# Head norms summed by rounds of three tiles, a stacked decay sum, and a memory attention by pairs of heads

## The chip, the cores and the metric

One core of a Trainium2 chip runs the kernel. The metric is the device time of one execution in microseconds (us); smaller is better. TensorE multiplies, VectorE, ScalarE and GpSimd work on tiles in SBUF and PSUM, and SyncE (SP) issues the loads of the weights.

## The reference, cut to what matters

Two blocks of a model over 512 tokens of width 1024, in f32. The first has three mixers (a state-space scan with decays per head, a gated recurrence, retention) and a feed-forward; the second has two layers with memory attention in both and multi-head latent attention in the second.

```python
def rms_norm(x, g):
    y = xf * lax.rsqrt(jnp.mean(xf * xf, axis=-1, keepdims=True) + EPS)
    return y * g
def memory_attention(q_mem, mem, mem_norm_g, w_mem_kv, g_q, g_k):
    q = rms_norm(q_mem.reshape(b, s, 4, 64), g_q)
    k, v = jnp.split(rms_norm(mem, mem_norm_g) @ w_mem_kv, 2, axis=-1)
    k = rms_norm(k.reshape(b, m, 4, 64), g_k)
    p = jax.nn.softmax(jnp.einsum('bqhd,bmhd->bhqm', q, k) * 64 ** -0.5, axis=-1)
    o = jnp.einsum('bhqm,bmhd->bqhd', p, v)
```

There are 256 memory tokens (m). The latent attention has 6 heads; for each, rms_norm is applied to the 128 plain features of keys and queries and to their 64 rotary ones, before rotation; the attention is causal over both parts.

The decay sums are the running sums of log decays of each of 16 heads along the tokens; the first block needs exp of their differences within a chunk of 128 tokens.

## The kernel before, in words

Activations lie as tiles of 128 features by 512 tokens. Every weight is f32 and is split in two f32r halves: ScalarE copies the raw panel to w_hi (L1366), VectorE (L1871) or GpSimd (L649) subtracts to get w_lo, and TensorE does three matmuls per block (L689 to L691). A panel is 128 by 1024, eight blocks; 525 panels are streamed by SP into four raw buffers, each load waiting for the low of the panel four before it; w_hi and w_lo have two buffers each, so ScalarE starts panel n when TensorE is done with panel n - 2. STAGES (L64 on) lists the stages with their panels, tiles and posting units. POOL_RUNS (L96) names the runs of panels whose lows GpSimd makes; VectorE makes the others. The order of all work on each engine is written out by hand in the four engine programs, and semaphores with counts join them. There is no planner.

PSUM has eight banks: 0 to 3 take the GEMM tiles in turn (bank_free waits until tile t - 4 was drained), 4 to 7 are the AUX banks, taken in turn by aux_tile (L768 on); aux_done, aux_used count their filling and use.

**Decay sums.** In stage ssd_y the sums of 16 heads stand in rows (acs, 16 by 512). They are split into acs_hi and acs_lo (VectorE, L2252), and spread(hd) (L949) broadcasts the row of one head over 128 partitions by two matmuls, one of each half, with a column of the identity (L954, L955). Two heads are spread between two gate panels; ScalarE and VectorE make the decay matrices from them.

**Small norms.** A head norm needs the mean of squares over the 128 or 64 features of a head, for each token. sums (L779) multiplies the squares of a tile, 128 tokens at a time as the stationary operand, by one column of ones (L788, two columns for 64-wide heads), so that the sums stand by token in a few columns. ScalarE takes the root of these columns (L1421), VectorE the reciprocal (L2007, 0.2 us), and spread_norms (L794) turns them back with the identity over the features (L804). VectorE multiplies the tile by gain and norm (L2013). ROUNDS (L140) lists ten rounds of two tiles in the second layer: keys, memory queries, queries, rotary parts, memory keys. Squares are ScalarE's there (L1414).

**First layer.** After conv0 the memory queries (qm0) are projected, then the norm of the memory itself, the panels of mem0 (four of 256 columns, the memory's keys and values), then conv, nine panels whose tiles VectorE combines in conv_part (L2535) by threes. Between them TensorE does the sums and spreads of the memory keys and of the memory queries, turns the values (L1124), and runs Attention: eight units, each one head by 256 queries. A unit is scores (L1131), maximum on VectorE (L2022), exponential on ScalarE (L1444), division on VectorE (L2041), transposition (L854), copy on ScalarE, and the values of a head after its two units (L1137). Unit u is done after conv panel u + 2; the last ones follow the last conv panel and stand in wo0's first tile.

**Second layer.** mla_in gives cq (three tiles) and the memory queries qm. ukv (three panels) gives keys and values of the six heads; the values are turned (L1222) in six PSUM tiles of a stage of their own. uq (five panels) gives six q_nope and three q_rope tiles, mem1 (four panels) the memory's keys and values. The rounds of norms stand between the panels. VectorE normalises the memory again (L2518 on), from a second sum of squares (ScalarE's eight squares, L1762, and TensorE's memory_sum1, L821) and makes the rotary tables (L2675 to L2685); ScalarE takes their sine (L1822). turn (L1227) does the rotation of a tile. Then pairs of heads run in STEPS: memory pairs and latent pairs by PairedHeads (L240), whose two heads use the two halves of the array's rows or columns (L1259, L1306).

Of the kernel before, what the change touches and what calls it, by code (L numbers as in the profile page):

```python
# [26 lines left out]
F32 = mybir.dt.float32  # L27
F32R = mybir.dt.float32r
# [56 lines left out]
def schedule():  # L85
    out, n, t, s = {}, 0, 0, 0
    for name, panels, tiles, units in STAGES:
# [9 lines left out]
             "conv": (ST["conv0"].n + 2, ST["wo0"].n), "s1a": (ST["s1a_in0"].n + 2, ST["s1a_in"].n - 1),  # L97
# [34 lines left out]
def split_runs():  # L132
# [7 lines left out]
ROUNDS = [["k0", "k1"], ["k2", "k3"], ["k4", "k5"], ["mq0_1", "mq1_1"], ["q0", "q1"], ["q2", "q3"], ["q4", "q5"],  # L140
          ["qr0", "qr1"], ["mk0_1", "mk1_1"], ["qr2"]]
SMALL_NORMS = [(f"m{w}{j}_0", 1, MEM_D, c, False, (2, 3)) for w, c in (("k", MEM), ("q", S)) for j in range(2)]
SMALL_NORMS += [("ckv", 2, 2 * P, S, False, (0, 1, 2, 3)), ("krope", 1, 64, S, False, (0, 1, 2, 3)),
                ("cq", 3, 3 * P, S, False, (0, 1, 2, 3))]
SMALL_NORMS += [(name, 1, P if name[1].isdigit() else 64, MEM if name[:2] == "mk" else S, True, (0, 1, 2, 3))
                for names in ROUNDS for name in names]

# [10 lines left out]
def small_norms():  # L158
    out, squared, rotation = {}, {True: DT, False: 0}, 0
    for rooted, (name, tiles, dim, cols, by_scalar, slots) in enumerate(SMALL_NORMS):  # L160
        n = SmallNorm()
        n.tiles, n.dim, n.cols, n.by_scalar, n.heads = tiles, dim, cols, by_scalar, P // dim if dim < P else 1
        n.slots = [slots[(rotation + j) % len(slots)] for j in range(tiles)]
        n.squared = [squared[by_scalar] + j + 1 for j in range(tiles)]
        n.rooted = rooted + 1
        first = 8 * (rooted % 8)
        n.stats = slice(first, first + n.heads * cols // P)
        rotation, squared[by_scalar] = rotation + tiles, squared[by_scalar] + tiles
        out[name] = n
    return out  # L170
# [32 lines left out]


class Attention:

    def __init__(self, sems, heads, chunks, u0, t0, width, scale, pairs, probs, p_tok, scores, turned, outs, lag, stat,
                 cat):
        (self.scored, self.max_ready, self.exp_done, self.prob_ready, self.pt_done, self.pt_copied, self.pv_done,
         self.pv_taken) = sems
        self.heads, self.chunks, self.u0, self.t0, self.width, self.scale = heads, chunks, u0, t0, width, scale
        self.pairs, self.probs, self.p_tok, self.scores, self.turned = pairs, probs, p_tok, scores, turned
        self.outs, self.lag, self.stat, self.cat = outs, lag, stat, cat
        self.per_head = CH // chunks
        self.n, self.ahead = heads * self.per_head, len(scores)  # L220

    def tile(self, hd):

        return (hd // 2, hd % 2 == 0, hd % 2 == 1) if self.pairs else (hd, True, True)

    def due(self, u, more):

        at_unit = [self.per_head * (hd + 1) + self.lag + more for hd in range(self.heads)]
        return [hd for hd, x in enumerate(at_unit) if x == u or u == self.n - 1 < x]

    def columns(self, u, which, e=None):

        c = self.stat + 4 * which + u * self.chunks % 4
        return slice(c, c + self.chunks) if e is None else slice(c + e, c + e + 1)

    def prob(self, u):
# [2636 lines left out]
```

## Time and profile before

| | |
|---|---|
| median of three runs | 3074.87 us (3074.26 to 3077.01) |
| the profiled execution | 3075.68 us |
| its span, first to last instruction | 3073.9 us |
| TensorE busy | 3027.8 us, 99% |
| VectorE, ScalarE, GpSimd busy | 59%, 31%, 8% |
| mean granted TensorE clock | 0.994 |
| HBM read | 283.96 MB, 93 GB/s |

The table is of the whole span. TensorE's time is that of its matmuls with their ends modelled, so that neighbours overlap; the spacing of their starts is what an edit changes.

### The profile page before, as it was taken

The numbers are of one execution on the slowest core, as the hardware profiler recorded it, in microseconds if no ns is written. First come the engines' busy times: TensorE is split into PE (matmuls) and PEld (weight loads), VectorE is DVE, ScalarE is ACT, GpSimd is POOL, SyncE is SP. The second block draws the span as 40 slices with busy tenths as digits, with TensorE's granted clock in tenths as the row PEclk, the third lists the DMA queues.
The fourth block names the chain that finished last, engine by engine and source line by source line (L and its number), as shares of the span: only waits on it lengthen the run. The fifth ranks groups of instructions, "written<-read, shape, count | busy, mean of one in ns | idle before, by whom it ended". The sixth has DMA issues, their size and how long they took to land.

```text
span 3073.9 us, 36959 instructions
## 1 busy us (share of the span) xinstructions
PE 3027.8 (99%) x13711; PEld 2467.5 (80%) x13711; DVE 1815.4 (59%) x2422; ACT 946.4 (31%) x1302; POOL 243.6 (8%) x111
## 2 busy tenths in 40 slices
PE   8999999999999999999999999999999999999999
PEld 7887788787888878888777888887888878688887
DVE  8896565667666555554666655445554447665532
ACT  4643632333222222222223222222222234422222
POOL 0043240000000000000142000002000022000000
PEclk9999999999999999999999999999999999999999
DMA  4222123233222222223321222332222321022222
GB/s 145 96 96 83 62 96 117 69 104 102 96 96 98 100 96 82 96 99 106 110 96 62 91 100 96 103 103 89 97 99 98 108 81 56 28 96 96 96 102 97
DMA packets 79309, 287.61 MB, mean 94 GB/s; under 512 B 8992, under 2 KB 9248, under 8 KB 78816
## 3 DMA queue, kind: packets, MB, share of 16 engines
q1 hardware_dynamic: 77904, 280.06, 27.1%
q0 software_dynamic: 1296, 6.03, 0.6%
q8 instruction: 76, 1.25, 0.2%
q14 instruction: 33, 0.27, 0.0%
HBM read 283.96 MB, written 2.10 MB: 93 GB/s over the span
## 4 chain that ended last, share of the span: by engine, by line
PE 85%; issue 9%; DVE 3%; POOL 2%; ACT 1%; DMA 0%; POOLq 0%; DVEq 0%; ACTq 0%
PE ps L689 26%; PE ps L690 26%; PE ps L691 26%; POOL w_lo L649 2%; PE ps L788 1%; PE ps L804 1%; PE ps L1071 1%; PE ps L1268 0%; PE ps L1319 0%; DVE w_lo L1871 0%; PE ps L1296 0%; ACT w_hi L1366 0%; PE ps L753 0%; PE ps L1271 0%; PE ps L1060 0%
## 5 line engine op out<-in xcount | busy, mean ns | idle before, releaser
L1366 ACT ACTIVATE w_hi<-raw 128x1024 fp32r<-128x1024 f32 x524 | 554.4, 1058 | 1366.5 <-PE ps L691 1366.2
L689 PE MATMUL ps<-h_hi,w_hi 128*128 128x512 f32 (+1 forms) x2379 | 934.3, 393 | 7.0 <-DVE w_lo L1871 3.3
L690 PE MATMUL ps<-h_lo,w_hi 128*128 128x512 f32 (+1 forms) x2379 | 924.3, 389 | 0.0
L691 PE MATMUL ps<-h_hi,w_lo 128*128 128x512 f32 (+1 forms) x2379 | 924.2, 389 | 0.0
L1871 DVE TENSOR_TENSOR w_lo<-raw,w_hi 128x1024 fp32r<-128x1024 f32 x430 | 525.8, 1223 | 470.6 <-ACT w_hi L1366 465.4
L689 PEld LDWEIGHTS ps<-h_hi,w_hi 128*128 128x128 f32 x2379 | 448.1, 188 | 111.9 <-issue 10.9
L691 PEld LDWEIGHTS ps<-h_hi,w_lo 128*128 128x128 f32 x2379 | 447.8, 188 | 92.6
L690 PEld LDWEIGHTS ps<-h_lo,w_hi 128*128 128x128 f32 x2379 | 448.1, 188 | 91.9 <-issue 2.2
L689 PE MATMUL ps<-mid_hi,w_hi 128*128 128x512 f32 x1208 | 471.6, 390 | 2.2 <-DVE mid_lo L1949 2.1
L690 PE MATMUL ps<-mid_lo,w_hi 128*128 128x512 f32 x1208 | 470.5, 389 | 0.0
L691 PE MATMUL ps<-mid_hi,w_lo 128*128 128x512 f32 x1208 | 470.4, 389 | 0.0
L649 POOL TENSOR_TENSOR w_lo<-raw,w_hi 128x1024 fp32r<-128x1024 f32 x94 | 236.2, 2513 | 953.4 <-ACT w_hi L1366 945.7
L689 PEld LDWEIGHTS ps<-mid_hi,w_hi 128*128 128x128 f32 x1208 | 227.2, 188 | 51.3 <-DVE mid_lo L1949 3.5
L691 PEld LDWEIGHTS ps<-mid_hi,w_lo 128*128 128x128 f32 x1208 | 227.1, 188 | 47.3
L690 PEld LDWEIGHTS ps<-mid_lo,w_hi 128*128 128x128 f32 x1208 | 227.2, 188 | 47.1 <-issue 0.2
L1944 DVE TENSOR_TENSOR stage<-ps,rstd 128x512 f32<-128x512 f32 x104 | 71.8, 691 | 233.7 <-PE ps L691 233.7
L1371 ACT ACTIVATE stage<-ps 128x512 f32<-128x512 f32 x107 | 63.6, 599 | 365.2 <-PE ps L691 352.1
L689 PE MATMUL ps<-br_hi,w_hi 128*128 128x512 f32 x256 | 101.5, 397 | 10.0 <-DVE br_lo L2083 7.9
L1944 DVE TENSOR_TENSOR tmp<-ps,rstd 128x512 f32<-128x512 f32 x73 | 50.4, 691 | 99.5 <-PE ps L691 99.3
L690 PE MATMUL ps<-br_lo,w_hi 128*128 128x512 f32 x256 | 100.6, 393 | 0.0
L691 PE MATMUL ps<-br_hi,w_lo 128*128 128x512 f32 x256 | 100.6, 393 | 0.0
L1692 ACT ACTIVATE tmp<-tmp 128x512 f32<-128x512 f32 x112 | 69.3, 619 | 72.0 <-DVE tmp L1967 58.2
(416 smaller groups left out, 2556.6 us busy)
## 6 DMA issues: line engine op xcount, KB each, us to landing
raw<-in_wstream SPq DMA_DIRECT2D x525, 512.0 KB, 3.3
x<-in_x SPq DMA_DIRECT2D x4, 512.0 KB, 6.4
x_in<-in_x POOLq DMA_DIRECT2D x8, 256.0 KB, 3.0
mem_x<-in_mem POOLq DMA_DIRECT2D x2, 1024.0 KB, 5.0
out<-x SPq DMA_DIRECT2D x8, 256.0 KB, 4.4
tmp<-in_ret_decay POOLq DMA_DIRECT2D x1, 1024.0 KB, 5.9
rope_r<-in_rope_r POOLq DMA_DIRECT2D x1, 512.0 KB, 4.0
mats<-in_mats SPq DMA_DIRECT2D x1, 256.0 KB, 8.3
```

The costliest lines, as they stand in the source:

```text
L649: nc.gpsimd.tensor_tensor(w_lo[:, n % HL], raw[:, n % RAW], w_hi[:, n % HL].bitcast(F32), ALU.subtract)\
L689: nc.tensor.matmul(dst, hi_w, hi_x, start=first, stop=False)
L690: nc.tensor.matmul(dst, hi_w, lo_x, start=False, stop=False)
L691: return nc.tensor.matmul(dst, lo_w, hi_x, start=False, stop=last)
L788: mm = nc.tensor.matmul(dst[:, n.heads * c:n.heads * c + n.heads], tmp[:, n.slots[j], P * c:P * c + P], ones, start=j == 0, stop=j == n.ti ...
L804: mm = nc.tensor.matmul(dst[rows, P * c:P * c + P], small[:, k:k + 1].to_broadcast([P, P // n.heads]), IDENT, start=True, stop=True)
L1071: mm = nc.tensor.matmul(bank(t)[:, P * c:S], v_tok[:, c, f:f + P], scores[:, hd % 2, OFF[c]:OFF[c] + WIDTH[c]], start=c == 0, stop=True, s ...
L1366: nc.scalar.activation(w_hi[:, n % HL], raw[:, r], ACT.Copy).then_inc(hi_ready, 1)
L1371: nc.scalar.activation(dst, src[rows, 0:cols], func, bias=bias, scale=scale).then_inc(drained, 1)
L1692: nc.scalar.activation(tmp[:, s % 2], tmp[:, s % 2], func).then_inc(act_done, 1)
L1871: v.tensor_tensor(w_lo[:, n % HL], raw[:, n % RAW], w_hi[:, n % HL].bitcast(F32), ALU.subtract)\
L1944: v.tensor_tensor(dst, bank(t), scale, ALU.mult).then_inc(drained, 1)
```

## The change

1. Decay sums: acs_hi and acs_lo become rows 0 to 15 and 32 to 47 of one tile of 64 rows, zero elsewhere, and a table pick2 of two stacked identities selects both at once: one matmul for a head.
2. Rounds: a round is three tiles. round_sums sums the squares over the partitions, with 32 columns of ones, into three groups of 32 partitions of one bank; ScalarE takes one root of 96 by 512, VectorE one reciprocal, and round_spread broadcasts them over the features in three banks, from three groups of 32 rows, six matmuls for 64-wide heads. Seven rounds: one in the first layer, six in the second. Memory keys (two tiles of 256) count as one tile.
3. First memory attention: PairedHeads in four steps, scores and first transposition in the middle of a conv panel.
4. Lows of memory panels 1 to 3 and of conv panel 0 go from GpSimd to VectorE; mem0's first low stays.
5. Second layer: the panels of uq and mem1 and the turned values are interleaved in one stage with the rotary query tiles earlier; the reciprocal root of the memory is kept from the first layer (L1762 and L821 go); rotary tables and sine come earlier; the AUX banks of the pairs are renamed.

Removed with them are the class Attention, sums of these tiles and spread_norms of them. The core of the diff, in the order of the file: tables, TensorE (helpers, first layer, second layer), ScalarE's root, VectorE (reciprocal, first layer, second layer):

```diff
-    ("mla_in", 5, 5, 0), ("ukv", 3, 12, 0), ("v_turned", 0, 6, 0), ("uq", 5, 9, 0), ("mem1", 4, 4, 0), ("wo1", 8, 8, 8),
+    ("mla_in", 5, 5, 0), ("ukv", 3, 12, 0), ("uq", 9, 19, 0), ("wo1", 8, 8, 8),
-             "conv": (ST["conv0"].n + 2, ST["wo0"].n), "s1a": (ST["s1a_in0"].n + 2, ST["s1a_in"].n - 1),
+             "conv0": (ST["conv0"].n + 2, ST["mem0"].n), "conv": (ST["conv"].n + 1, ST["wo0"].n), "s1a": (ST["s1a_in0"].n + 2, ST["s1a_in"].n - 1),
+MEM1_PANEL, MEM1_TILE = (2, 3, 7, 8), (10, 11, 17, 18)
+UQ_PANEL, UQ_TILE = (0, 1, 4, 5, 6), (2, 3, 6, 7, 12, 13, 14, 15, 16)
+V_TILE = (0, 1, 4, 5, 8, 9)
+ROUNDS = [["mq0", "mq1", "mk"], ["k0", "k1", "k2"], ["k3", "k4", "k5"], ["mq0", "mq1", "mk"], ["qr0", "qr1", "qr2"], ["q0", "q1", "q2"],
+          ["q3", "q4", "q5"]]
...
+            def round_sums(r):
+                dst, heads = aux_tile(), len(ROUNDS[r])
+                ones = ONES[:, 0:32] if by_head(r) else mat["ones64"][:, 48:80]
+                pe.wait_ge(act_squared, DT + heads * r + heads)
+                for j in range(heads):
+                    mm = nc.tensor.matmul(dst[32 * j:32 * j + 32, :], ones, square_slot[square_of(r, j)], start=True, stop=True)
                 mm.then_inc(aux_done, 1)
+            def round_spread(r):
+                pe.wait_ge(aux_used, sum_at[r])
+                dst = [aux_tile() for _ in ROUNDS[r]]
+                wide = P if by_head(r) else 64
+                for first in range(0, P, wide):
+                    for j in range(len(ROUNDS[r])):
+                        rows, one = slice(32 * j, 32 * j + 32), 32 * j + first // 4
+                        mm = nc.tensor.matmul(dst[j][first:first + wide, :], IDENT[rows, one:one + 1].to_broadcast([32, wide]),
+                                              rows_rstd[r % 2][rows], start=True, stop=True)
...
-                nc.tensor.matmul(dst, sel, acs_hi[:], start=True, stop=False)
-                nc.tensor.matmul(dst, sel, acs_lo[:], start=False, stop=True).then_inc(bcast_done, 1)
+                nc.tensor.matmul(spread_bank(hd), pick2[:, hd:hd + 1].to_broadcast([64, P]), acs2[:], start=True, stop=True)\
+                    .then_inc(bcast_done, 1)
...
+            round_sums(0)
+            for j in range(2):
+                memory_turned(ST["mem0"].t + 3 + j, mem_vt, j)
             conv_part(ST["conv"], 1)
+            round_spread(0)
+            def middle(j):
+                if j == 5:
+                    first_values(1)
+                if j < 6:
+                    first_scores(j - 2)
+                if 3 <= j < 7:
+                    first_turned(j - 3, 0)
+                if j == 7:
+                    first_values(3)
+            for j in range(2, 9):
+                conv_part(ST["conv"], j, middle=(lambda: middle(j)) if j < 8 else None)
+                if 3 <= j < 7:
+                    first_turned(j - 3, 1)
...
+            round_sums(1)
+            v_turned_tiles(0)
+            uq_gemm(0)
+            round_spread(1)
+            round_sums(2)
+            v_turned_tiles(2)
+            uq_gemm(1)
+            round_spread(2)
+            v_turned_tiles(4)
+            mem1_gemm(0)
+            mem1_gemm(1)
+            uq_gemm(2)
+            round_sums(3)
+            uq_gemm(3)
+            round_spread(3)
+            round_sums(4)
+            uq_gemm(4)
+            round_spread(4)
+            round_sums(5)
             turn(krope[:, 0])
+            mem1_gemm(2)
+            round_spread(5)
+            round_sums(6)
+            normalised(4)
+            turn(q_rope[:, 0])
+            mem1_gemm(3)
+            round_spread(6)
...
+                nc.scalar.activation(rows_rstd[r % 2], ps[0:96, AUX + (aux[0] - 1) % 4], ACT.Sqrt, bias=eps_col[0:96],
+                                     scale=1.0 / (P if by_head(r) else 64)).then_inc(rows_rooted, 1)
...
+                v.reciprocal(rows_rstd[r % 2], rows_rstd[r % 2]).then_inc(aux_used, 1)
...
+            split(ST["mem0"].n + 1)
             conv_part(ST["conv1"], 2, 2, 2)
-            for j in range(4):
+            for j in range(1, 4):
                 split(ST["mem0"].n + j + 1)
+            conv_part(st, 3, 0, 3)
+            round_reciprocal(0)
+            for j in range(2):
+                memory_values(mem_v, j)
             conv_part(st, 3, 1, 3)
+            round_norms(*memory_gain("q", 0), qm[:, 0], qm[:, 1])
+            round_norms(*memory_gain("k", 0), mem_k_whole)
...
+            rotary_table(0, 0.25)
+            rotary_table(1, 0.0)
+            reciprocals("cq")
+            memory_input(1, mem_x1, spare[:, 0], mem1_hi, mem1_lo, range(0, 4))
+            small_norm("cq", [cq[:, k] for k in range(3)], [vcol("g_q_lora_2", k) for k in range(3)])
+            for k in range(3):
+                halves(cq_hi[:, k], cq_lo[:, k], cq[:, k], lat_ready if k == 2 else None)
+            round_reciprocal(1)
+            memory_input(1, mem_x1, spare[:, 0], mem1_hi, mem1_lo, range(4, 8))
+            round_norms(gk, *(k_nope[:, hd] for hd in range(3)))
+            round_reciprocal(2)
+            round_norms(gk, *(k_nope[:, hd] for hd in range(3, 6)))
+            round_reciprocal(3)
+            round_norms(*memory_gain("q", 1), qm[:, 0], qm[:, 1])
+            round_norms(*memory_gain("k", 1), mem_k1_whole)
+            round_reciprocal(4)
+            round_norms(gr, *(q_rope[:, j] for j in range(3)))
+            round_reciprocal(5)
+            turn(krope[:, 0])
+            round_norms(gq, *(q_nope[:, hd] for hd in range(3)))
+            round_reciprocal(6)
+            turn(q_rope[:, 0])
+            round_norms(gq, *(q_nope[:, hd] for hd in range(3, 6)))
```

## Rows read from the trace of the kernel before

**Rows 1.** The page: busy time, two groups of part 5, an issue of part 6
```profile
PE 3027.8 (99%) x13711; PEld 2467.5 (80%) x13711; DVE 1815.4 (59%) x2422; ACT 946.4 (31%) x1302; POOL 243.6 (8%) x111
...
L1871 DVE TENSOR_TENSOR w_lo<-raw,w_hi 128x1024 fp32r<-128x1024 f32 x430 | 525.8, 1223 | 470.6 <-ACT w_hi L1366 465.4
...
L649 POOL TENSOR_TENSOR w_lo<-raw,w_hi 128x1024 fp32r<-128x1024 f32 x94 | 236.2, 2513 | 953.4 <-ACT w_hi L1366 945.7
...
raw<-in_wstream SPq DMA_DIRECT2D x525, 512.0 KB, 3.3
```

**Rows 2.** Windows: start:end, length, busy us of PE, PEld, DVE, ACT, POOL, clock, DMA
```profile
294.88:364.80 69.92, 69.92 (x398) 52.01 (x398) 38.56 (x68) 50.08 (x118) 17.17 (x7) 1.00 0.17 54
...
1570.64:1677.65 107.01, 97.15 (x494) 75.84 (x492) 64.58 (x102) 30.34 (x65) 32.71 (x13) 0.95 0.20 68
...
2495.83:2597.42 101.59, 98.04 (x686) 85.52 (x684) 57.17 (x98) 47.00 (x87) 29.53 (x12) 0.98 0.20 67
```

**Rows 3.** Windows of two stretches at the lower clock, same columns
```profile
1579.90:1586.70 6.80, 4.74 (x22) 4.74 (x23) 4.80 (x2) 0.47 (x1) 4.52 (x2) 0.50 0.37 122
1607.20:1610.60 3.40, 3.26 (x10) 2.71 (x11) 1.46 (x6) 1.41 (x2) 2.37 (x1) 0.50 0.01 2
```

**Rows 4.** TensorE's waits, 1570 to 1678: us in total, times, longest
```profile
PE ps L689 <- POOL w_lo L649: 6.2, 3, 4.3
```

**Rows 5.** Timeline, TensorE: start, us, engine, line; 256 and 512 columns
```profile
1587.00 0.28 PE L689 MATMUL ps<-mem_hi,w_hi 128*128 128x256 f32 x1
...
1587.36 0.28 PE L689 MATMUL ps<-mem_hi,w_hi 128*128 128x256 f32 x1
...
2488.35 0.39 PE L689 MATMUL ps<-h_hi,w_hi 128*128 128x512 f32 x1
...
2489.03 0.39 PE L689 MATMUL ps<-h_hi,w_hi 128*128 128x512 f32 x1
```

**Rows 6.** Timeline, TensorE: from one pair's first spread to the next work
```profile
308.50 0.49 PE L954 MATMUL ps<-acs_hi,ident_r 16*128 16x512 f32 x1
...
309.63 0.50 PE L689 MATMUL ps<-h_hi,w_hi 128*128 128x512 f32 x1
```

**Rows 7.** Chain that ended last, in order of time: start, us, what
```profile
420.22 0.86 PE ps L753 x2
...
1625.83 1.06 PE ps L1131 x4
...
1648.38 1.86 PE ps L1137 x4
...
2612.20 1.87 PE ps L1306 x8
...
2614.44 1.06 PE ps L1259 x8
```

**Rows 8.** Timeline of VectorE, GpSimd and ScalarE at six places
```profile
2466.53 3.35 DVE L1938 RECIPROCAL rstd<-rstd 128x512 f32<-128x512 f32 x1
...
1572.38 2.59 DVE L2546 TENSOR_TENSOR cpad<-tmp,stage 128x512 f32<-128x512 f32 x1
...
2517.68 1.75 DVE L2511 RECIPROCAL rstd<-rstd 128x256 f32<-128x256 f32 x1
...
2517.09 2.93 POOL L649 TENSOR_TENSOR w_lo<-raw,w_hi 128x1024 fp32r<-128x1024 f32 x1 [9.40 <-ACT w_hi L1366]
...
2588.09 1.28 ACT L1822 ACT_TABLE_LOAD   x1
2589.39 1.06 ACT L1822 ACTIVATE rope<-rope 128x1024 f32<-128x1024 f32 x1
```

**Rows 9.** Groups of TensorE from 2495.8 to 2597.4: busy us, mean ns
```profile
L788 PE MATMUL ps<-mats,tmp 128*128 128x1 f32 (+1 forms) x168 | 19.7, 247 | 0.0
...
L804 PE MATMUL ps<-mats,small 128*128 128x128 f32 (+1 forms) x200 | 19.0, 276 | 0.6 <-DVE small L2007 0.6
```

**Rows 10.** Timeline, VectorE: the first score maximum of the second layer
```profile
2597.42 0.68 DVE L2709 TENSOR_REDUCE small<-ps 128x2 f32<-128x512 f32 x1
```

More of the change, by code:

```diff
@@ L202, in col @@
     return vec[:, c:c + 1] if i is None else vec[:, bass.ds(i * step + c, 1)]
[L205 to L236, printed above, removed]
-        return self.probs[:, u % self.probs.shape[1]]
 class PairedHeads:
@@ L829, in att_start @@
-            def att_start(a, score, tiles):
-                pe.wait_ge(aux_used, aux[0])
-                pe.wait_ge(rms_done, norms[0])
-                pe.wait_ge(drained, tiles)
-                for u in range(a.ahead):
-                    att_scores(a, score, u)
-            def att_value(a, value, hd):
-                tile, first, last = a.tile(hd)
-                pe.wait_ge(a.pt_copied, a.u0 + a.per_head * (hd + 1))
-                if first and tile >= len(a.outs):
-                    pe.wait_ge(a.pv_taken, a.t0 + tile - len(a.outs) + 1)
-                mm = value(a.outs[tile % len(a.outs)], hd)
-                if last:
-                    mm.then_inc(a.pv_done, 1)
@@ new lines, in side_rows, with memory_scores @@
+            def side_rows(side):
+                return slice(64 * side, 64 * side + 64)
+            def memory_scores(a, keys, k, dst):
+                j = a.pair(k)
+                for e in range(2):
+                    for side in range(2):
+                        mm = nc.tensor.matmul(dst[side][:, MEM * e:MEM * e + MEM], qm[side_rows(side), j, a.queries(k, e, 1)],
+                                              keys[side_rows(side), j], start=True, stop=True)
+                        if e == 1:
+                            mm.then_inc(a.scored, 1)
@@ L1722, in _, with memory @@
                     memory_root(spare[:, 0])
-            def memory(l, k, v_in, behind=None):
+            def memory(l, k, v_in):
                 st = ST[f"mem{l}"]
@@ new lines, in uq_drain, with mem1_drain, drained_up_to @@
+            def uq_drain(g):
+                n = st.n + UQ_PANEL[g]
+                split(n + 1)
+                for k in range(2 * g, min(2 * g + 2, 9)):
+                    drain(n, st.t + UQ_TILE[k], q_rope[:, k - 2] if 2 <= k < 5 else q_nope[:, k if k < 2 else k - 3])
+            def mem1_drain(j):
+                n = st.n + MEM1_PANEL[j]
+                split(n + 1)
+                drain(n, st.t + MEM1_TILE[j], mem_k1[:, j] if j < 2 else mem_vt1[:, j - 2], cols=MEM)
+            def drained_up_to(tile):
+                act.wait_ge(drained, st.t + tile + 1)
```

599 lines of the change are left out of this document (241 added, 358 removed).

## The prediction

> **What bounds the kernel now.** I read the page's busy line first: TensorE is busy 99% of the span [rows 1], so a change is worth what it takes off TensorE's own queue, plus or minus TensorE's waits. Then the windows of the three stretches that are edited [rows 2]: the spread of the decay sums, from 294.88; the memory GEMMs and the first attention, from 1570.64 to the second output tile of wo0 at 1677.65; and the second layer's norms, from ukv at 2495.83 to the first score maximum at 2597.42 [rows 10]. TensorE is busy all of the first, 97.15 of 107.01 us of the second and 98.04 of 101.59 us of the third. The granted clock falls in the second: 6.8 us from 1579.9 and 3.4 us from 1607.2 stand at half speed [rows 3], which costs (6.8+3.4)/2 = 5.1 us. TensorE is idle for 107.01 - 97.15 = 9.9 us there, 6.2 of them waiting for weight lows made by GpSimd [rows 4].
>
> A spacing is what TensorE pays: for a weight block of 512 columns 0.68 us by its three matmuls, so 5.46 us a panel of eight; with 256 columns 0.36 us, so 2.9 us a panel [rows 5]. An f32 matmul of the code stands as two records.
>
> **Decay sums.** Each pair of heads issues four matmuls in 1.13 us, from 308.50 to 309.63 [rows 6]. Each streams 0.23 us; the remaining 0.2 us lies at the ends, where the array's row grouping changes. Two matmuls leave 1.13 - 0.46 = 0.67 us. Eight pairs give **-3.7 us**. The fill and the pick table (VectorE, some 0.5 us) come before spread(0), which is due only about 1 us after the lows are ready: hidden; at worst +0.5. ScalarE is busy 50.08 of 69.92 us [rows 2], so it need not become the bound.
>
> **Overlap of narrow matmuls.** Nothing in the trace runs three at once; it shows two. Scores of one head take 1.06 us for four records, of two heads on alternate row halves 1.06 us for eight; values of one head take 1.86 us for four records, of two heads on alternate column halves 1.87 us for eight [rows 7]. A plain f32 matmul of 512 columns takes 0.86 us [rows 7]. So a round's sum (three matmuls on three column groups) costs between 1.0 us (all at once, with 0.1 for the change of grouping) and 3 x 0.86 = 2.6 us (one by one); its spread the same, for 64-wide heads (six matmuls) 1.5 to 5.2 us. I take 1.0, 1.0 and 1.5, as the rows with two are twice as fast to within 0.01 us.
> The Trainium skill, "TensorEngine Tiling (Array Packing)", Key Properties, says that different tiles can execute in parallel, and its table of speedups goes to four for a dimension of 32 or less. By it the low ends hold; by the pair rows alone, read as a limit of two, a round's sum would be 1.7 to 1.9 us. No row here shows three.
>
> **First attention.** TensorE's new content from 1570.64: four memory panels 11.9, nine conv panels and one tile of wo0 54.6, round sum 1.0, two turned values 0.6, round spread 1.5, four paired scores 4 x 1.06 = 4.2, eight transpositions as before 4.2, two paired values 3.7: together 81.7 us. Old content: the same GEMMs 66.5, scores 8 x 1.06, values 4 x 1.86, transpositions 4.2, and sums, spreads and turned values of some 6.2, so 92.8 us; with 9.9 idle and 5.1 of slow clock that is 107.8, against 107.0 measured.
> The waits, laid out in queue order. Lows of memory panels 1 to 3 and of conv panel 0 leave GpSimd (2.51 us [rows 1], and it blocks VectorE's SBUF work: a product took 2.59 us beside it where others take 0.7 [rows 8]) for VectorE (1.23 us [rows 1]). But the first is queued behind a conv part: VectorE's product, scale and two taps end at 1575.0, the low at 1576.3, so memory panel 1, with panel 0 done at 1573.6, waits 2.8 us. The low of panel 2 is ready at 1579.9: 0.7 us. Conv panel 0 starts at 1586.0 instead of 1591.04. Round 0: sum at 1591.4, root, and then a reciprocal of 512 columns, 3.35 us [rows 8], in place of 0.18 us ones: done at 1596.8, the spread at 1598.5 doesn't wait. VectorE then does conv part (3,1), one of its operations held 2.3 us by GpSimd, and three norms: ready at 1606.6, while the first scores stand ready at 1602.7: **a new wait of 4.0 us**. Behind the waiting scores stand the rest of conv panel 2 and all later panels. Later steps have 7 us a panel for a chain of 4 us; wo0 waits some 0.4. Waits total 7.9, against 9.9. So 81.7 + 7.9 = 89.6, tile 1 of wo0 at 1660.2: -17.4 us. I add one half-clock stretch of 3.4 us, 1.7 us, where the old had three: **-15.7**.
>
> **Second layer.** The old stretch holds 168 records of column sums and 200 of spreads [rows 9]; 19.7 + 19.0 = 39 us with the parts for cq; the memory's square sum is some 3 more. New content: ukv 18.1 with its half-clock stretch as before, cq's sum and spread 3.5, six round sums 6.0, four spreads of 1.0 and two of 1.5, six turned v tiles 3.2, nine uq tiles 18.4, four memory panels 11.9, two rotary turns 1.9, one turned value 0.3: 70.3 us. ScalarE's eight squares and the sum for the memory go (the reciprocal root of the first layer is reused), off the path but for 3.3 us of TensorE.
> VectorE's queue decides the waits. The rotary tables (16 operations, 10 to 12 us with one or two GpSimd holds) now stand ahead of cq, as do four memory tiles (4.7 us), so cq's lows end at 2522.6. ScalarE's sine moves before uq's first split: table 1.28 and sine 1.06 us [rows 8]; it delays that panel's hi, which is ready anyway, and the table returns before root 1. The six reciprocals add 6 x 3.35 = 20 us. In order, TensorE waits: round sum 1 for squares 0.9; uq panel 0 for cq 2.3; spread 2 for its reciprocal, behind memory tiles and three norms, 4.4; memory panel 1 for its low 1.3; uq panel 3 for a drain 0.9; spread 4 2.6, spread 5 0.7, spread 6 2.2 for their reciprocals. That is 15.3 us. Scores 0 start at 2495.8 + 70.3 + 15.3 = 2581.4. VectorE then still turns one rotary tile, norms three and copies one (after the reciprocal ended at 2580.0): first maximum at 2584.4, with old 2597.42: -13.0; the loose ends of the queues take 0.7, so -12.3. One more half-clock stretch, 1.7: **-10.6**. What follows (pairs) has the same steps and is moved whole; a value copy between two maxima costs 0.4 at most.
> SP's loads wait for lows as before; four loads ahead at 3.3 us each [rows 1] cover panels of 3 to 5.5 us. Unrolled loops of SP and GpSimd: nothing.
>
> **Sum.** 3.7 + 15.7 + 10.6 = 30.0. The profiled execution took 3075.68 us; the median of the three runs is 0.8 below it. 3075.68 - 30.0 = 3045.7, median-like **3045**.
>
> **Rivals.**
> A. *Three narrow matmuls don't overlap.* With 0.86 each the second layer is 2.8 us slower than now, the first attention gains 15.9, decay 3.7; with 3.4 for the clock -13.4: 3062. Against: the pair rows. Chance 0.10.
> B. *Slower: each narrow f32 matmul also empties the array before the next group's.* Place: the 51 matmuls of the seven rounds. At 1.2 us each the gain is 1.7 less 3.4 for the clock, about nothing; each 0.1 us more costs 5.1. At 1.4 us each: +8 to +10, 3084. It decides from 1.3 us. Against: alternate halves show no such price [rows 7]. Chance 0.03, and 0.03 for a price near 1.2, no change.
> The Tiling page of the Trainium skill, Key Properties, says that changing the tiling mode, not just the tile, drains the engine; by that B would not occur, only one entry and exit a round. The 0.2 us of rows 6 fit that.
> C. *VectorE is later still.* If reciprocals were held by GpSimd too, 1.2 us each, the second layer's waits grow by 5: 3050 to 3052. Against: a reciprocal of 256 columns at 2517.68 took its 1.75 us while GpSimd was on [rows 8]. Chance 0.16.
> D. *Fewer waits than laid out and no half-clock stretches.* 3.4 back and half of the 15.3 covered: 3034 to 3037. Chance 0.12.
> E. *The change of lows does nothing*, as VectorE only swaps the wait: panel 0 of conv at 1590 instead of 1586: 3049, inside the range.
>
> **How the numbers follow.** Forecast with E 0.56. The range 3033 to 3063 leaves out B and the tails. A measurement tells 0.2%, 6 us, from no change. Faster by more: all but B and a little, 0.94; within 0.03; slower 0.03.
>
> **What would show it.** In the profile after: decay pairs of 0.67 us; round sums and spreads near 1.0 us (2.6 shows A); conv panel 0 near 1586; waits before the first scores of about 4 us and before spread 2 of about 4, both ended by VectorE; records on TensorE fewer by some 450; first maximum of the second layer 13 us earlier relative to ukv. Wrong if a wait over 5 us stands in either stretch, or if half clock covers over 20 us more.

## The result, and the profile after

The changed kernel takes **3041.84 us** (median of four runs, 3039.88 to 3043.62), the kernel before, run between them on the same chip, 3075.57. The ratio is 0.989, its 95% interval 0.9873 to 0.9907: 34 us less. Timed again beside three of the experiments, the changed kernel took 3042.61 against 3074.76, ratio 0.9894 (0.9877 to 0.991). The forecast was 3045, the range 3033 to 3063. The profiled execution took 3040.44 us with a span of 3038.2; the span of before was 3073.9.

The page of the changed kernel: busy time of each engine, and the two groups of lows [rows 1].

```profile
PE 2986.5 (98%) x13373; PEld 2418.5 (80%) x13373; DVE 1828.8 (60%) x2405; ACT 943.8 (31%) x1279; POOL 231.7 (8%) x107
...
L1846 DVE TENSOR_TENSOR w_lo<-raw,w_hi 128x1024 fp32r<-128x1024 f32 x434 | 530.7, 1223 | 473.9 <-ACT w_hi L1344 473.1
```

TensorE has 338 records fewer and 41.3 us less busy time, but the span fell by 35.7: the rest became waiting. The windows of the same three stretches [rows 2] (start:end, length, busy us of PE, PEld, DVE, ACT, POOL, granted clock, DMA share, GB/s) are these.

```profile
294.74:367.72 72.98, 72.62 (x414) 54.41 (x413) 41.20 (x73) 51.69 (x121) 19.87 (x8) 1.00 0.16 53
1565.92:1658.16 92.24, 85.17 (x440) 66.00 (x438) 64.06 (x98) 31.59 (x64) 21.95 (x9) 0.96 0.24 79
2474.88:2562.61 87.73, 76.04 (x412) 54.18 (x410) 68.24 (x82) 45.83 (x72) 28.99 (x12) 0.94 0.23 77
```

The second line was 107.01 us long and is 92.24; the third was 101.59 and is 87.73. In the third TensorE was idle 3.6 us and is idle 11.7 now, although the stretch is 13.9 shorter: the part took off more than 20 us of work and gave 8 back in waits. The first window is cut later than the one of before, by which the stage with the decay sums ended at 370.96; now it ends at 367.72.

The table places the whole difference by where stretches begin and end in the two traces.

| where | before | after | difference |
|---|---|---|---|
| end of the stage with the decay sums | 370.96 | 367.72 | -3.24 |
| up to memory panel 0 (a half-clock stretch at 1173.7 is absent) | 1570.64 | 1565.92 | -4.72, so -1.5 more |
| memory GEMMs and first attention | 107.01 | 92.24 | -14.77 |
| between (a half-clock stretch at 2129.4 is absent) | 818.18 | 816.72 | -1.46 |
| second layer up to the first maximum | 101.59 | 87.73 | -13.86 |
| pairs of heads up to wo1 | 69.28 | 68.66 | -0.62 |

They sum to 35.4 of 35.7 us. Half clock means a granted clock of 0.50 in the rows, 1.2 GHz, the lower of TensorE's two levels. The two absent stretches, 3.0 us, stand where the programs agree, each behind a wait that both kernels have (2.06 us, ended at 1173.8 in the kernel before and at 1170.5 in the changed one, and 1.88 us, ended at 2128.4 and at 2108.9). They are no part of the change and come and go from run to run: in the second profile of the changed kernel half clock stands at 1144.0 and 1171.3, and the memory panels start at 1568.10 instead of 1565.92.

The new waits of TensorE in the second stretch, and then in the third (engine, tile, line, what it waited for: us in total, times, longest), are:

```profile
PE ps L822 <- DVE mem_k L2024: 3.7, 1, 3.7
PE ps L663 <- DVE w_lo L1846: 3.3, 2, 2.8
```

```profile
PE ps L809 <- DVE ckv L2019: 6.5, 3, 3.6
PE ps L663 <- issue: 2.0, 1, 2.0
PE ps L797 <- DVE krope L2649: 1.2, 1, 1.2
PE ps L663 <- POOL w_lo L622: 0.7, 2, 0.4
PE ps L1101 <- issue: 0.7, 1, 0.7
PE ps L797 <- ACT stage L1392: 0.6, 1, 0.6
```

L822 are the scores, L809 the spreads of a round, L797 its sums, L663 the GEMMs, L1101 a turned tile. Where GpSimd's lows ended 6.2 us of waiting before [rows 4], VectorE's norms and lows end 7.0 now.

TensorE's timeline shows what the narrow matmuls cost (start, us, engine, line, tiles, count): a decay pair, then round 0's sum, then its spread of six matmuls.

```profile
302.77 0.73 PE L935 MATMUL ps<-acs,pick 64*128 64x512 f32 x2
303.43 1.13 PE L957 MATMUL ps<-xw_tok,b_tok 128*128 128x512 f32 x2
...
1587.63 0.62 PE L797 MATMUL ps<-tmp,mats 128*32 128x512 f32 x2
1587.64 0.62 PE L797 MATMUL ps<-acc,mats 128*32 128x512 f32 x1
1588.08 0.60 PE L797 MATMUL ps<-tmp,mats 128*32 128x512 f32 x2
1588.09 0.59 PE L797 MATMUL ps<-acc,mats 128*32 128x512 f32 x1
1588.62 0.33 PE L1101 MATMUL ps<-mats,mem_vt 128*128 128x128 f32 x1
...
1594.69 1.10 PE L809 MATMUL ps<-ckv,mats 32*64 32x512 f32 x12
1595.72 0.50 PE L663 MATMUL ps<-h_hi,w_hi 128*128 128x512 f32 x1
```

A pair takes 303.43 - 302.77 = 0.66 us instead of 1.13 [rows 6]. In the sum, the first records of all three matmuls start within 0.01 us at 1587.63, the second records at 1588.08, and the next work at 1588.62: 0.99 us for three matmuls of 0.86 each. The six of the spread take 1.03 us.

### The profile page after: what moved, and what is told of

The parts are those of the page before. It is cut to its first block, busy times and chain, and to the rows that moved or that the text cites. A ratio compares the mean times of both kernels' runs of the same rounds, so it can differ in the third digit from the quotient of the medians.

```text
span 3038.2 us, 36195 instructions
## 1 busy us (share of the span) xinstructions
PE 2986.5 (98%) x13373; PEld 2418.5 (80%) x13373; DVE 1828.8 (60%) x2405; ACT 943.8 (31%) x1279; POOL 231.7 (8%) x107
## 4 chain that ended last, share of the span: by engine, by line
PE 83%; issue 10%; DVE 5%; POOL 2%; ACT 1%; DMA 0%; POOLq 0%; ACTq 0%; DVEq 0%
PE ps L663 26%; PE ps L665 26%; PE ps L664 26%; POOL w_lo L622 2%; PE ps L1052 1%; PE ps L1297 0%; DVE w_lo L1846 0%; PE ps L1260 0%; DMA mem_x<-in_mem 0%; ACT w_hi L1344 0%; PE ps L833 0%; PE ps L727 0%; PE ps L1041 0%; DVE small L1997 0%; PE ps L947 0%
## 5 line engine op out<-in xcount | busy, mean ns | idle before, releaser
L663 PE MATMUL ps<-h_hi,w_hi 128*128 128x512 f32 (+1 forms) x2379 | 935.1, 393 | 8.7 <-DVE w_lo L1846 3.3
L663 PEld LDWEIGHTS ps<-h_hi,w_hi 128*128 128x128 f32 x2379 | 448.4, 188 | 115.7 <-issue 13.5
L663 PE MATMUL ps<-mid_hi,w_hi 128*128 128x512 f32 x1208 | 470.8, 390 | 2.2 <-DVE mid_lo L1924 2.1
L622 POOL TENSOR_TENSOR w_lo<-raw,w_hi 128x1024 fp32r<-128x1024 f32 x90 | 224.3, 2493 | 939.8 <-ACT w_hi L1344 931.8
L663 PEld LDWEIGHTS ps<-mid_hi,w_hi 128*128 128x128 f32 x1208 | 226.8, 188 | 50.8 <-DVE mid_lo L1924 3.5
L663 PE MATMUL ps<-br_hi,w_hi 128*128 128x512 f32 x256 | 101.8, 398 | 9.7 <-DVE br_lo L2060 7.7
```

The lines of the kernel that those rows point to most:

```text
L622: nc.gpsimd.tensor_tensor(w_lo[:, n % HL], raw[:, n % RAW], w_hi[:, n % HL].bitcast(F32), ALU.subtract)\
L663: nc.tensor.matmul(dst, hi_w, hi_x, start=first, stop=False)
```

## The experiments

All were made from the changed kernel; the diffs are cut to their core. Two measures are used beside the medians: the memory stretch, from memory panel 0 to the second output tile of wo0 (92.24 us, in its second profile 92.26), and the norm stretch, from the first column sum of cq (2480.34) to the first maximum (82.27, in its second profile 83.33). A median of the changed kernel is 3041.84 or 3042.61, and its single runs lie between 3039.88 and 3043.62, so that a part worth 1 us shows in its place and not in a median. The second profile of the changed kernel has the waits of the first at the same places, but half clock at other ones.

### The decay sum in two matmuls again

```diff
-nc.tensor.matmul(spread_bank(hd), pick2[:, hd:hd + 1].to_broadcast([64, P]), acs2[:], start=True, stop=True)
+nc.tensor.matmul(dst, sel, acs_hi[:], start=True, stop=False)
+nc.tensor.matmul(dst, sel, acs_lo[:], start=False, stop=True)
```

> The change without its decay part: each decay spread is again two matmuls, of the high half and of the low half. My theory (the seven later pairs of spreads stand in TensorE's line with nothing beside them): a pair of spreads goes from 0.66 back to 1.13 us, the stage with the heads ends 3.2 to 3.7 us later, and the kernel takes 3.2 to 3.7 us more than the changed one, with everything behind it only moved. Rival (the vector work of the stage sets its end, and TensorE would wait there for as long as it saved): the pair is 1.13 us again but the stage ends less than 1 us later.

Measured: a pair takes 1.13 us (294.38 to 295.51), the stage runs from 294.38 to 370.46, 3.1 us longer than the 294.74 to 367.72 of the changed kernel, and memory panel 0 starts 2.66 us later. The median is 3043.23. The stage comes within 0.1 us of the theory's 3.2 to 3.7 and the rival falls. The medians differ by 0.6 to 1.4 us only, where the expectation had 3.2 to 3.7: in the total this part is not shown, as half-clock stretches at other places move the medians by as much.

### Round sums one by one

```diff
-for j in range(heads):
+for j in range(heads if by_head(r) else 0):
+    mm = nc.tensor.matmul(dst[0:96, :], shifted[:, 64 - 32 * j:160 - 32 * j], square_slot[square_of(r, j)],
+                          start=j == 0, stop=j == heads - 1)
+for j in range(0 if by_head(r) else heads):
     mm = nc.tensor.matmul(dst[32 * j:32 * j + 32, :], ones, ..., start=True, stop=True)
```

> The sums of the four rounds whose heads are 128 wide (rounds 1, 2, 5, 6) are made by three full-height matmuls that add up in one bank, each with its ones shifted to its 32 columns, so that no two can run beside each other; the values are the same. My theory (three matmuls in three column groups of 32 run beside each other, which is why a sum took 0.99 us): a sum takes 2.5 to 2.7 us, 1.6 more each, 6.4 in all, of which 4 to 6.4 us show in the total, since a longer sum also starts the root and the reciprocal behind it later, while the waits in front of uq0 and of round sum 6 take in some. Rival (a sum is short because its matmuls write only 32 rows, and not because they overlap): a full-height one differs from it too, so that the length alone would not tell; what tells is the spacing of the starts, 0.02 to 0.1 us inside a sum now and 0.86 us in this kernel.

Here shifted is a tile of zeros with 32 columns of ones, so that each matmul writes all 96 rows and the three add up in one bank.

Measured: 3046.19 us, 3.6 to 4.4 more than the changed kernel, and a norm stretch of 87.30 (2479.46 to 2566.76), 4.0 to 5.0 longer. TensorE's timeline of round sum 1 here:

```profile
2496.50 1.07 PE L797 MATMUL ps<-tmp,fill 128*96 128x512 f32 x2 [0.63 <-ACT stage L1395]
2497.41 1.88 PE L797 MATMUL ps<-stage,fill 128*96 128x512 f32 x4
2499.13 1.04 PE L1213 MATMUL ps<-mats,q_nope 128*128 128x128 f32 x8
2500.74 0.47 PE L663 MATMUL ps<-h_hi,w_hi 128*128 128x512 f32 x1 [0.57 <-issue]
```

The sum now takes 2499.13 - 2496.50 = 2.63 us for the same three inputs, with starts 0.9 us apart, where those of the changed kernel are 0.01 us apart. Running beside each other is thus what makes a sum 0.99 us. Four sums are 6.6 us longer and not all of it shows: the wait at uq0, behind the sum, fell from 1.97 to 0.57, that at spread 2 from 3.58 to 1.99. Rival A of the prediction had this for every round.

### The two heads in turn

```diff
-for e in range(2):
-    for side in range(2):
+for side in range(2):
+    for e in range(2):
```

and the same exchange in the values.

> The memory attentions with the same matmuls in another order: both halves of the scores of one head and then both of the other, and likewise the four value matmuls of one head and then those of the other (before and after the change the heads alternate matmul by matmul). My theory (the two heads' matmuls lie in different halves of the array, and run beside each other only when they stand next to each other in the queue): scores go from 1.06 to about 1.7 to 2.1 us a step and values from 1.87 to about 3.0 to 3.7, with 8 steps of each in the two layers together 10 to 22 us, of which the last value step of one head may still overlap the next thing. Rival (the queue looks past its head, so order does not matter): scores and values as before, and the total within 1 us.

Measured: 3040.49 us, memory stretch 92.30. Scores 1.08 us, values 1.87: nothing changed. **The theory was wrong in its condition.** That the two heads overlap isn't touched, since one head's two value matmuls alone took 1.86 us in the kernel before [rows 7] and four take 1.87 here; but they need not alternate.

### In turn, with a wait between

```diff
 for side in range(2):
+    pe.wait_ge(a.pt_copied, a.count(k, 1))
     for c in range(MEM // P):
```

> As the kernel with the heads in turn, with one more wait on a semaphore long reached, between the value matmuls of the first head and those of the second, so that the order in which they are handed to TensorE is certain. Theory (TensorE starts a record that waits for nothing in its own half of the array while earlier ones still run in the other half, up to some records ahead): a value step again takes 1.87 us. Rival (in the earlier experiment the matmuls had been brought back into alternating order before they reached TensorE): 2.6 to 3.5 us a value step, as the wait holds the order.

Measured: 3041.67 us, and this value step in TensorE's timeline:

```profile
1628.14 1.94 PE L842 MATMUL ps<-p_tok,mem_v 128*64 128x512 f32 x8
1630.02 1.14 PE L822 MATMUL ps<-mem_k,qm 64*128 64x256 f32 x8
```

1630.02 - 1628.14 = 1.88 us. Eight records (four of one head, then four of the other) still take the time of four. The trace bears out that the program kept its edit: two of the step's weight loads carry the wait, and in both kernels with the heads in turn the first records of the two heads start 13 to 14 ns apart, where they start 6 ns apart when the heads alternate. The rival, alternating order brought back ahead of TensorE, is thus very unlikely, though no row shows the queue itself. It is then TensorE that starts the second head's records beside the first's. How far ahead it does so was not tried beyond these four records.

### The four lows on GpSimd again

```diff
-"conv0": (ST["conv0"].n + 2, ST["mem0"].n), "conv": (ST["conv"].n + 1, ST["wo0"].n)
+"conv": (ST["conv0"].n + 2, ST["wo0"].n)
```

> The change without the move of the four lows: those of memory panels 1 to 3 and of convolution panel 0 of the last channel tile are made by GpSimd again, at 2.9 us each, instead of VectorE. My theory (GpSimd's chain of lows, 2.9 us each, stands ahead of these panels, and with TensorE's work in between made shorter it would be late): memory panels 1, 2 and 3 wait for it, convolution panel 0 starts 3 to 5 us later than in the changed kernel, and since VectorE is relieved of 4 x 0.6 us and of the waits for the highs, the first scores wait less than 3.75 us; net 1 to 4 us slower. Rival (the lows are no bound once the round is short): memory panel 1 waits as now, convolution panel 0 starts within 0.5 us of now, and the total is within 1 us or even lower, since VectorE's norms for the first scores come sooner.

The list of runs that GpSimd makes is back to one run from conv0 on.

Measured: 3045.93 us, 3.3 to 4.1 more. The waits of its memory stretch (96.91 us, from 1566.33):

```profile
PE ps L662 <- POOL w_lo L622: 5.8, 3, 4.3
PE ps L821 <- DVE mem_k L2023: 3.7, 1, 3.7
PE ps L662 <- DVE w_lo L1845: 0.5, 1, 0.5
```

Convolution panel 0 starts 20.68 us after memory panel 0 instead of 16.13. The 5.8 us are nearly the 6.2 of before [rows 4]. Rival E (moving the lows does nothing) falls. The wait of the scores did not shrink, against what I had expected: it is counted from the round sum, which came as much later as the panels did.

### Three orders of VectorE's queue

Norms of round 0 ahead of a convolution part:

```diff
-conv_part(st, 3, 1, 3)
 round_norms(*memory_gain("q", 0), qm[:, 0], qm[:, 1])
 round_norms(*memory_gain("k", 0), mem_k_whole)
...
         maxima(mem_first, j - 2, side, FIRST_SCORES[side])
+    if j == 2:
+        conv_part(st, 3, 1, 3)
```

> In VectorE's queue the norms of round 0 (memory queries and keys) stand before the second part of convolution tile 3, which goes behind the first pair's maxima. My theory (the 3.75 us at the first scores are VectorE's: the reciprocal of 3.35 us, a conv part, one operation of it held by GpSimd, and three norms): the wait at the first scores falls to 0.5 to 1.5 us, the part is still in time for its panel, and the kernel takes 2 to 3.5 us less. Rival (the reciprocal alone makes the lateness): the wait stays above 2.5 us and the total falls by less than 1.2 us.

The lows of memory panels 1 and 2 ahead of the taps:

```diff
-conv_part(ST["conv1"], 2, 1, 2)
-split(ST["mem0"].n + 1)
-conv_part(ST["conv1"], 2, 2, 2)
-for j in range(1, 4):
+for part in (1, 2):
+    scaled(ST["conv1"].n + part, ST["conv1"].t + part, stage[:, part - 1])
+split(ST["mem0"].n + 1)
+conv_part(ST["conv1"], 2, 1, 2, False)
+split(ST["mem0"].n + 2)
+conv_part(ST["conv1"], 2, 2, 2, False)
+for j in range(2, 4):
```

(False leaves out the part's own low and scaling, which stand above.)

> First layer: the low of memory panel 1 is made by VectorE before the product and the taps of the convolution part that stands ahead of it now, and the low of panel 2 between the two parts. My theory (the 2.81 us at memory panel 1 are VectorE's queue order): the wait goes, convolution panel 0 starts 2.3 to 2.9 us sooner. How much of it is left at the first scores depends on VectorE: it does the same work before the norms, and the round sum comes sooner, so 1.5 to 2.8 us in total. Rival (the round's chain through VectorE decides anyway): the wait at the first scores grows from 3.75 to about 6.4 and the total stays.

Two memory tiles of the second layer behind reciprocal 2 (ScalarE's wait for these tiles moves with them):

```diff
 round_reciprocal(1)
-memory_input(1, mem_x1, spare[:, 0], mem1_hi, mem1_lo, range(4, 8))
+memory_input(1, mem_x1, spare[:, 0], mem1_hi, mem1_lo, range(4, 6))
 round_norms(gk, *(k_nope[:, hd] for hd in range(3)))
 round_reciprocal(2)
+memory_input(1, mem_x1, spare[:, 0], mem1_hi, mem1_lo, range(6, 8))
```

> Second layer: two of the four memory tiles that VectorE normalises ahead of norms 1 go behind the second reciprocal. My theory (spread 2 waits for reciprocal 2 because 2.3 us of memory tiles stand ahead of it): the wait at spread 2 falls from 3.58 to about 1.3 us; half or more of it comes back at memory panel 1 or at spreads 3 to 5, since VectorE's queue holds the same work up to the first maximum, so the stretch to the first maximum gains 0 to 2 us. Rival (a wait removed in the middle is a gain in full): 2.3 us less in total.

The changed kernel was timed again beside these three.

> The changed kernel itself, timed again beside the next three. All theories: 3038 to 3044 us, with the places of its waits as in its first profile.

| kernel | median | range of runs | its stretch |
|---|---|---|---|
| changed, again | 3042.61 | 3041.22 to 3043.44 | 92.26 and 83.33 |
| norms first | 3038.09 | 3035.51 to 3041.94 | memory 88.18 |
| lows first | 3039.12 | 3037.89 to 3041.82 | memory 89.47 |
| memory tiles later | 3039.27 | 3038.51 to 3039.49 | norm 80.46 |

**Norms first.** The wait of 3.75 us at the first scores is gone and 1.31 us stand at the first transposition instead, as VectorE's queue now has the part between maxima and division: -2.4 us of waiting, and what remains is within the 0.5 to 1.5 us expected. The stretch is 4.1 us shorter, the other 1.7 being a half-clock stretch that is absent, so the median fell by 3.8 to 4.5, more than the 2 to 3.5 expected. Its four runs are spread widely, and the profiled one is the slowest, 3041.94: its memory panels start only at 1570.08, with half clock at 1146.5 and 1173.8 ahead of them, so that the gain shows in the stretch and in the median and not in the span of this profile. VectorE's timeline shows why the wait was there (changed kernel: start, us, line, operation).

```profile
1589.46 3.35 DVE L2019 RECIPROCAL ckv<-ckv 96x512 f32<-96x512 f32 x1 [1.03 <-ACT ckv L1397]
1592.73 0.68 DVE L2503 COPY mem_v<-ps 128x256 f32<-128x256 f32 x2
1594.80 0.69 DVE L1919 TENSOR_TENSOR stage<-ps,rstd 128x512 f32<-128x512 f32 x1 [1.39 <-PE ps L665]
1595.52 0.69 DVE L2524 TENSOR_TENSOR cpad<-tmp,stage 128x512 f32<-128x512 f32 x1
1596.25 2.50 DVE L1938 TENSOR_SCALAR tmp<-cpad,vec 128x512 f32<-128x512 f32 x1
1598.78 1.54 DVE L1942 SCALAR_TENSOR_TENSOR tmp<-cpad,vec,tmp 128x512 f32<-128x512 f32 x2
1600.36 1.41 DVE L2024 SCALAR_TENSOR_TENSOR qm<-qm,vec,ps 128x512 f32<-128x512 f32 x2
```

The reciprocal is done at 1592.8 and the spread at 1595.7, but the norms (L2024) start at 1600.36, behind a conv part that is held once, 2.50 us at 1596.25, while GpSimd makes a low from 1595.99 to 1598.47 (the same operation takes 0.49 us in norms first, where GpSimd is idle). The rival, that the reciprocal alone makes the lateness, falls.

**Lows first.** Memory panels 1 and 2 wait 0.45 and 0.83 us instead of 2.81 and none; convolution panel 0 starts 13.35 us after memory panel 0 instead of 16.13, so 2.78 sooner. The wait at the scores stays at 3.75 and does not grow, since the whole chain behind the round sum moved forward with the panels. The memory stretch is 2.8 us shorter, of which 1.5 are waits and the rest is the clock (one half-clock stretch, at 1599.9, instead of two). Its rival falls.

**Memory tiles later.** Spread 2 waits 1.23 us instead of 3.58; 0.80 us appear at memory panel 0, where none stood, and 1.70 stand at panel 1, where 0.3 to 1.2 stood. In all TensorE is idle for 80.46 - 69.34 = 11.1 us of the stretch, where it was 11.7 and 12.8 in the two profiles of the changed kernel, so that of the 2.35 us taken off at spread 2 some 0.7 to 1.8 came back as other waits; the theory had half or more, the rival none. The stretch gains 1.8 to 2.9 us all the same, and the median 2.6 to 3.3, which alone would suit the rival (2.3 in full): the rest is the clock, two half-clock stretches instead of three.

All three together:

> The three reorderings of VectorE's queue together: norms of round 0 before the second part of tile 3, lows of memory panels 1 and 2 ahead of the taps, two memory tiles of the second layer behind reciprocal 2. My theory (three different waits, of which each alone gave 1.5 to 2.5 us on TensorE, in different places): they add up, 4 to 6.5 us less than the changed kernel, so 3036 to 3038 us, or down to 3033 where a half-clock stretch also falls away. Rival (the first two stand in one chain, so that the second only moves the wait of the first): 3 to 4 us less.

Measured: **3032.71 us** (3032.58 to 3033.28), 0.9861 of the kernel before (0.9845 to 0.9878), and 9.1 to 9.9 us less than the changed kernel. The memory stretch, its waits, and the norm stretch:

```profile
1568.72:1654.16 85.44, 82.33 (x440) 63.64 (x438) 62.61 (x98) 31.60 (x64) 22.54 (x9) 1.00 0.25 86
```

```profile
PE ps L663 <- DVE w_lo L1847: 1.8, 3, 0.8
PE ps L833 <- DVE probs L2009: 1.3, 1, 1.3
```

```profile
2473.11:2552.86 79.75, 67.58 (x388) 47.71 (x386) 62.88 (x77) 44.44 (x71) 26.36 (x11) 0.98 0.23 78
```

The memory stretch is 6.8 us shorter than 92.24, as 4.1 and 2.8 alone had given; 7.07 - 3.1 = 4.0 of it are waits and the rest is the clock, 0.96 before and 1.00 now. The rival, that the second exchange only moves the wait of the first, falls. The norm stretch is 2.5 to 3.6 us shorter, but TensorE is idle for 79.75 - 67.58 = 12.2 us of it, against 11.7 and 12.8: what this exchange gives here is the clock, one half-clock stretch instead of three, and not waiting. So the times add up, but the theory's reason for it, three waits that go, holds for the first two; the third wait goes and comes back at other places. The total went 0.3 us beyond the 3033 that was named for a half-clock stretch that falls away. Outside the last 2 us half clock covers 17.1 us of this profile and 23.9 and 27.3 of the changed kernel's two, so that some 3 to 5 of the 9.1 to 9.9 us are the clock.

## Why the prediction was right

**Decay sums: -3.7 forecast, -3.24 measured.** The pair was put at 0.67 us and takes 0.66. Eight pairs at 0.47 are 3.8; one new wait of 0.36 us for VectorE's decay tile at 314.31 took its part back. VectorE's decay was there the next bound, where the text had looked at ScalarE alone.

**Overlap: the low ends of the prices held.** 1.0 us for a round sum was measured at 0.99, 1.0 for a spread of three at 1.06. The spread of round 0, put at 1.5, took 1.03: the six 64-wide matmuls run beside each other all at once and not three and three. Rival A, 2.6 us a sum, is what the serial experiment gave, and B, 1.2 us and more per narrow matmul, is refuted by the same rows. The Trainium skill, "TensorEngine Tiling (Array Packing)", Key Properties, has different tiles executing in parallel; the trace agrees, with 0.99 us for three and 1.03 for six.

**First attention: -15.7 forecast, -14.77 measured.** Waits were laid out as 2.8, 0.7, 4.0 and 0.4, together 7.9; measured were 2.81, none, 3.75 and 0.51, together 7.07. Convolution panel 0 was to come 15.4 us after memory panel 0 and came after 16.13. TensorE's work is 92.24 - 7.07 less the 3.4 us that two half-clock stretches cost, so 81.8 against 81.7. The whole miss of 0.9 is the clock, one stretch more (1.7), less the waits (0.8). Windows of the changed kernel that show the two stretches, which begin 0.4 us ahead of them, at 1572.4 and 1603.1:

```profile
1572.80:1576.20 3.40, 3.40 (x19) 0.55 0.41 149
1603.50:1606.90 3.40, 3.40 (x12) 0.55 0.00 0
```

**Second layer: -10.6 forecast, -13.86 measured.** This is the term that was off. Its work on TensorE was right: from ukv to the first scores 85.95 us, less waits 11.7 and 3.4 of additional half clock, is 70.9 against 70.3. The waits were put 3.6 us too high, 15.3 against 11.7: spread 2 at 4.4 (3.58), spread 4 at 2.6 (2.17), memory panel 1 at 1.3 (0.33), uq3 at 0.9 (0.42); and spread 6 at 2.2, where none stands, since 1.23 us of it are taken two places ahead, at round sum 6, which waits for VectorE's rotation of krope, a dependence that the layout had not seen. The same late work was counted at the end again: VectorE was to hold the first maximum until 3.0 us after the first scores, and it came after 1.78; the 0.7 us added for loose ends were not there either. The clock went the other way, 3.4 us where 1.7 was put. In sum -3.6 + 0.6 + 1.7 - 1.9 = -3.2.

**Pairs of heads: 0 forecast, -0.62 measured.** The step "the same steps, moved whole" hides two things, which the windows from the first latent scores to the values of the first memory pair show, before and after:

```profile
2600.42:2612.13 11.71, 10.48 (x44) 7.89 (x45) 10.77 (x34) 6.31 (x22) 0.00 (x0) 0.56 0.00 1
```

```profile
2565.60:2576.16 10.56, 6.79 (x44) 4.70 (x44) 10.07 (x30) 5.68 (x20) 0.00 (x0) 1.00 0.01 2
```

Before, 10.2 us at half clock stood there from 2600.5; they are gone, and the same 44 records take 3.7 us less. But TensorE is idle 3.8 us there instead of 1.2: it waits 1.64 and 0.41 us for the probabilities and, new, 1.72 us for the last rotated query tile. So the slow clock before lay over work which would have waited, and 2.5 of its 3.7 us came back as waits. Ahead of this stretch the wait of 3.45 us is 0.69 now because the rotation of two query tiles stands in its place (1.88 us); from the first maximum to the first latent scores it is 3.0 us in both.

**The signs and the rivals' sums.** The waits named, about 4 us at the first scores and at spread 2, came as 3.75 and 3.58, both ended by VectorE. Records were to be fewer by some 450 and are fewer by 338: this count was wrong and bears on no time. The sum behind rival B doesn't come out of its own rule: 1.7 us of gain at 1.2 us a matmul, less 3.4 for the clock and 5.1 for each further 0.1, is 12 us slower at 1.4 us, not 8 to 10. How rival A's 15.9 us for the first attention come about is not worked out in it.

**Rival C** had reciprocals held by GpSimd. VectorE's timeline in the second layer shows a cast and the reciprocal of round 2:

```profile
2504.94 2.35 DVE L1851 CAST h_hi<-acc 128x256 fp32r<-128x256 f32 x1
...
2513.19 3.34 DVE L2019 RECIPROCAL ckv<-ckv 96x512 f32<-96x512 f32 x1
```

and GpSimd's the two lows beside them:

```profile
2504.74 2.40 POOL L622 TENSOR_TENSOR w_lo<-raw,w_hi 128x1024 fp32r<-128x1024 f32 x1 [6.31 <-ACT w_hi L1344]
2512.47 2.36 POOL L622 TENSOR_TENSOR w_lo<-raw,w_hi 128x1024 fp32r<-128x1024 f32 x1 [5.34 <-ACT w_hi L1344]
```

The cast takes 2.35 us beside the first low, where the next ones of its size take 0.29; the reciprocal takes 3.34 beside the second, as it does alone [rows 8]. C is refuted. Rival D (half the waits covered, no half clock) went partly true in the waits and not in the clock. The sum against the profiled execution was 3045.7. It became 3040.44 by -3.3 from the second layer, -3.0 from the two stretches absent outside the change, -0.6 from the pairs, +0.9 and +0.5 from the other two parts and 0.2 that is not placed. The 3.0 us are luck, and so, in part, is the good total: the miss in the second layer and the two small ones go different ways. The median of the changed kernel lies 1.4 us above its profiled execution, hence 3041.84.

Not tried: the first attention with one head a step again, which would be the direct price of pairing. That part rests on the rows: eight scores of 1.06 us became four, and four values of 1.86 us became two. Nor was the new order of the second layer (item 5 of the change) taken back by itself, or the reuse of the memory's root: that stretch is explained by counting work and waits in the trace, not by removal.

## What to carry to other kernels

Where matmuls are narrow, count groups and not matmuls: three sums (0.99 us) or six spreads (1.03) in different parts of the array cost little more than the 0.86 us of one. With two heads of two matmuls each the order of the records in the queue made no difference. Work taken off the bounding engine shortens the time in which the other engines had hidden, so lay out their queues before the change is made: here more than 20 us of work less made 8 us of waits in the second layer, and three exchanges in VectorE's queue that add no instruction then gave 9 us. A wait of some us costs more than itself where a stretch at half clock follows it, and an exchange that only splits a long wait into shorter ones can pay by the clock alone.

## What the runs showed of the hardware that was not expected

- **TensorE overlaps records out of turn.** Two heads' value matmuls, queued as four records of one and then four of the other, with a wait between that had been met, take 1.88 us, where they take 1.86 to 1.87 when they alternate; one head's four alone take 1.86.
- **Six f32 matmuls at once.** Three row groups by two column halves, 512 columns each, took 1.03 us; one plain matmul takes 0.86.
- **Half clock behind a wait.** In the changed kernel the 2.81 us wait that ends at 1571.77 is followed by a stretch at the lower of the two levels from 1572.4, and the 3.75 us wait that ends at 1602.48 by one from 1603.1, each 3.4 us long and so 1.7 us dear. Without the wait at the scores (norms first) the second is absent, without the long one at the panels (lows first) the first, and with both removed the stretch has clock 1.00. The twelve profiles together have 27 waits of TensorE of 2.8 us and more after the first 300 us, and at each of them half clock begins, from 2.1 us before to 1.5 us after its end. Behind shorter waits it comes in some runs and not in others: all twelve have waits of 1.82, 2.06 and 1.88 us near 1143, 1169 and 2108, and half clock begins at them in four, six and two. Some stretches have no wait over 0.6 us ahead of them (2446.2, among column sums of one column each, and 2483.8 in the changed kernel); what decides there is open.
- **A reciprocal of 512 columns isn't held by GpSimd** (3.34 us beside a low), while a cast (2.35 us instead of 0.29) and a TENSOR_SCALAR (2.50 instead of 0.49) are, by some 2 us each.
